# Moving the tiles of normed rows by 64 bytes in SBUF in a two-block transformer kernel

## The chip, the cores and the metric

The kernel runs on one core of one Trainium2 chip. The metric is the time of one execution on the device in microseconds, taken as the median of several runs.

## The reference

The input is a sequence of 256 rows of 1,024 numbers, all in 32-bit floating point. Two blocks follow one another, each with two layers of weights of its own.

```
def first_block(x, ...):
    for i in range(2):
        h = rms_norm(x, ln_attn_g[i])
        dq, dk, dv, mq, mk, mv = jnp.split(h @ w_in[i], cuts, axis=-1)
        ...
        x = x + jnp.concatenate([y_diff, y_moba], axis=-1) @ w_out[i]
        x = x + conv_ffn(rms_norm(x, ln_ffn_g[i]), w_up[i], conv_w[i], conv_b[i], w_down[i])
    return x

def second_block(x, c, ctx, ...):
    xc = ctx
    for l in range(2):
        h_l = _rmsnorm(x, g_pre[l]) * (1.0 + sc_l) + sh_l
        h_c = _rmsnorm(xc, g_pre[l]) * (1.0 + sc_c) + sh_c
        pl = _split_proj(h_l @ w_in[l])
        pc = _split_proj(h_c @ w_in[l])
        ...
        out_l = _mixer_output(pl, att_l, gla_l, *shared)
        if not last:
            out_c = _mixer_output(pc, att_c, gla_c, *shared)
            xc = xc + gt_c * _rmsnorm(out_c, g_post[l])
        x = x + gt_l * _rmsnorm(out_l, g_post[l])
    return x
```

In the first block `conv_ffn` multiplies the normed rows by `w_up` (1,024 by 5,632), applies a short convolution along the rows and a gated product, and multiplies by `w_down` (2,816 by 1,024). In the second block 256 rows of context go beside the 256 rows of the sequence through a wide projection into three branches (a convolution, an attention, a gated linear attention); in its second layer only the sequence's rows go on to the branches' outputs.

## The kernel before

Every large product is made on TensorE from numbers that were split in two: a number is rounded to the short form `float32r` (the "high" half), and the difference is the "low" half. A product is three matmuls: high by high, low rows by high weights, high rows by low weights.

Weights come in units of 512 KB (128 partitions by 1,024 numbers) by DMAs on SP's queue into the ring `RAW` (five slots). ScalarE rounds a unit into `SPH` (line 1559), and VectorE subtracts to make `SPL` (line 2132); both have four slots of 1,024 numbers. Rows are split into pairs of tiles:

- `HTH` and `HTL`, eight tiles (one per 128 of the 1,024 features) of 512 rows each, hold the normed rows, transposed, and later the attention output and the sum of the branches. With 256 rows in use, the slices are 256 columns long; with sequence and context together, 512.
- `ABH` and `ABL`, of the same shape, hold the inputs of the second block's branch products.
- `AH` and `AL`, three slots of 256 numbers, hold the gated product of the feed-forward stage, whose inner product with `w_down` is the function `down`.
- `RT` and `WDEC` are rows and weights of the low-rank decay product (line 1299).

Two functions of `tensor_program` make the products with HTH and HTL. `turned` (lines 1073 to 1075) loads a weight tile as the stationary side and streams 256 or 512 columns of rows, over eight tiles of features: 24 matmuls. `straight` (lines 1086 to 1088) loads 128 columns of rows as the stationary side and streams 512 columns of weights.

```
        for kt in kts:
            xh, xl = rows(src, kt)
            T.matmul(o, wh[:, kt, :], xh[:, kt, n0:n1], start=kt == 0, stop=False)
            T.matmul(o, wh[:, kt, :], xl[:, kt, n0:n1], start=False, stop=False)
            m = T.matmul(o, wl[:, kt, :], xh[:, kt, n0:n1], start=False, stop=kt == 7)
```

`down` (lines 1252 to 1254) does the same as `straight` with AH and AL as the stationary side, 12 matmuls for each of 22 tiles of features in each layer. In the profile's rows the tile that is named first after the arrow is the moving side, and the second is the stationary side. `rank` (lines 1263 and 1264) is a product of two of the three, with 512 columns.

Where a product's rows come from, `rows` decides (line 1052): HTH and HTL, or ABH and ABL for the three branch inputs. The order of the work on all engines is a list of steps that a planner writes ahead, from the program alone; addresses have no part in it.

The tiles' addresses are set in `build`: `put(name, off, shape)` places a tile at `base + off` in every partition, with `base` 16,512 (129 times 128), and returns the next free offset, rounded up to 32 bytes. RAW, SPH, SPL, HTH and HTL stand first, one behind the other, and all begin at a multiple of 128: SPH at 36,992, SPL at 53,376, HTH at 69,760, HTL at 86,144, each a multiple of 512 and 128 more. The offset `D` behind HTL is where all others are counted from. ABH stands at 188,224 and ABL at 204,608 (64 past a multiple of 128), AH at 212,832 and AL at 215,904 (96 past), RT at 204,608 and WDEC at 219,968 (64 past).

Of the kernel before, what the change touches and what calls it, by code (L numbers as in the profile page):

```python
# [7 lines left out]
F32R = mybir.dt.float32r  # L8
# [2829 lines left out]
def sync_program(sp, k):  # L2838
    D, sb, sched, s = sp.eng, k.sb, k.sched, k.signals

    def start():
        for t in range(2):
            D.dma_start(sb["XS"][:, t, 0:512], k.args["x"][0, t * 128:(t + 1) * 128, 0:512]).then_inc(
                *sp.tick(s["x_in0"]))

    def start2():
        for t in range(2):
            D.dma_start(sb["XS"][:, t, 512:1024], k.args["x"][0, t * 128:(t + 1) * 128, 512:1024]).then_inc(
                *sp.tick(s["x_in1"]))

    def load(u):
        name, idx, cols, kind = sched.order[u]
        p = u - NR
        if p >= 0 and sched.order[p][3] == "raw":
            sp.wait_ge(s["mm"], ("w", p))
        elif p >= 0:
            sp.wait_ge(s["hi"], ("u", p))
            sp.wait_ge(s["lo_" + sched.ready[p][1]], ("u", p))
        D.dma_start(sb["RAW"][:, u % NR, 0:cols], k.args[name][idx, :, 0:cols]).then_inc(
            *sp.tick(s[f"raw{u % NR}"], ("u", u)))  # L2860

    def finish():
        for t in range(2):
            for half, name in enumerate(("xa", "x")):
                c = slice(half * 512, half * 512 + 512)
                sp.wait_ge(s["out_dve"], (name, 1, t))
                D.dma_start(k.out[0, t * 128:(t + 1) * 128, c], sb["XS"][:, t, c]).then_inc(*sp.tick(s["out"]))
        sp.wait_ge(s["out"], 64)
        sp.wait_ge(s["spill0"], 32)
        sp.wait_ge(s["spill1"], 32)  # L2870

    does = {"start": start, "start2": start2, "load": load, "finish": finish}
    for step, *a in sched.steps:
        if step in does:
            does[step](*a)
# [6 lines left out]
def build(nc, args, out):  # L2882
    base = 16512
# [12 lines left out]
    m = Map()  # L2896
    o = m.put("RAW", 0, [128, 5, 1024])
    o = m.put("SPH", o, [128, 4, 1024], F32R)
    o = m.put("SPL", o, [128, 4, 1024], F32R)
    o = m.put("HTH", o, [128, 8, 512], F32R)  # L2900
    o = m.put("HTL", o, [128, 8, 512], F32R)
    D = o

    o = m.put("IDENT", D, [128, 128])
    o = m.put("PAR", o, [128, NPAR])
    o = m.put("TRI", o, [128, 384])
    o = m.put("MASK", o, [128, 7 * 128], U8)
    o = m.put("MODT", o, [128, 2, 24, 2])
    o = m.put("GP", o, [128, 2, 8, 2])
    o = m.put("CS", o, [128, 2, 16])  # L2910
    o = m.put("RS", o, [128, 3, 32])
    o = m.put("SS", o, [128, 8])
    o = m.put("GSS", o, [128, 2, 16])
    o = m.put("SSO", o, [128, 2, 4])
    o = m.put("AR", o, [128, 3, 4])
    o = m.put("ONE", o, [128, 1])
    o = m.put("BG", o, [128, 24])
    o = m.put("GC", o, [128, 2, 8])
    o = m.put("ROPE", o, [128, 2, 2, 2, 128])
    o = m.put("GN", o, [128, 2, 128])  # L2920
# [52 lines left out]
    p = m.put("YN", C + 16384, [128, 2, 1024])  # L2973
    p = m.put("QKN", p, [128, 2, 2, 512])
    p = m.put("VN", p, [128, 2, 1024])
    qkt_at = p
    p = m.put("QKT", p, [128, 8, 256])
    p = m.put("QP0", p, [128, 8, 256])
    p = m.put("BIAS", p, [128, 12, 256])
    m.put("MASKF", p, [128, 7 * 128])  # L2980
    p = m.put("E3", p, [128, 4, 384])
    m.put("DG1", p, [128, 2, 128])
    p = m.put("PT3", p, [128, 2, 384])
    p = m.put("XN1", p, [128, 2, 1024])
    p = m.put("SQ", p, [128, 2, 512])
    p = m.put("AROW1", p, [128, 256])
    p = m.put("SQY", p, [128, 512])
    p = m.put("QSY", p, [128, 2, 4])
    p = m.put("QS", p, [128, 2, 16])
    p = m.put("RR", p, [128, 4, 32])  # L2990
    p = m.put("SM", p, [128, 16])
    p = m.put("LT", p, [128, 64])
    p = m.put("LAMR", p, [128, 512])
    p = m.put("CSP", p, [128, 8, 32])
    p = m.put("SEL", p, [128, 2, 2])
    p = m.put("SE", p, [128, 2])

    m.put("FT", m.put("FC", qkt_at, [128, 2, 2, 256]), [128, 2, 256])
    p = m.put("AH", p, [128, 3, 256], F32R)
    p = m.put("AL", p, [128, 3, 256], F32R)  # L3000
    p = m.put("QP1", p, [128, 8, 256])
# [137 lines left out]
```

## Time and profile before

| | |
|---|---|
| median of 3 runs | 2103.14 us (2101.63 to 2103.3) |
| the profiled execution | 2102.27 us, span 2100.5 us |
| TensorE matmuls busy | 2053.5 us, 98% |
| TensorE weight loads busy | 1784.2 us, 85% |
| VectorE (DVE) busy | 1356.4 us, 65% |
| ScalarE (ACT) busy | 961.0 us, 46% |
| GpSimd (POOL) busy | 138.7 us, 7% |
| DMA | 285.79 MB, mean 136 GB/s |
| TensorE's granted clock | 0.994 of full speed |

The span goes from the first instruction to the last; the execution's time has a little at both ends beside it. Busy times of matmuls and weight loads overlap each other, and a matmul's duration holds a part in which the next one is already under way. So the price of a matmul in a dense stretch is read from the distance between the starts of two neighbours, in the timeline. By time, the stretches are: first block, layer 0 to 340 us and layer 1 to 680 us, each with projections and attention first and the feed-forward stage (147 to 340, 485 to 680) behind; second block, layer 0 to about 1560 us with 512 rows, and layer 1 from there with 256 rows in most products.

### The profile page before, as it was taken

The numbers are of one execution on the slowest core, as the hardware profiler recorded it, in microseconds if no ns is written. First come the engines' busy times: TensorE is split into PE (matmuls) and PEld (weight loads), VectorE is DVE, ScalarE is ACT, GpSimd is POOL, SyncE is SP. The second block draws the span as 40 slices with busy tenths as digits, with TensorE's granted clock in tenths as the row PEclk, the third lists the DMA queues.
The fourth block names the chain that finished last, engine by engine and source line by source line (L and its number), as shares of the span: only waits on it lengthen the run. The fifth ranks groups of instructions, "written<-read, shape, count | busy, mean of one in ns | idle before, by whom it ended". The sixth has DMA issues, their size and how long they took to land.

```text
span 2100.5 us, 31396 instructions
## 1 busy us (share of the span) xinstructions
PE 2053.5 (98%) x12082; PEld 1784.2 (85%) x12082; DVE 1356.4 (65%) x2381; ACT 961.0 (46%) x1576; POOL 138.7 (7%) x142
## 2 busy tenths in 40 slices
PE   9999999999999999999999999999999989999998
PEld 6788898878999888888888788888878889888997
DVE  6766667668777238567445556868565588575665
ACT  5655555655555434353332453233344454445443
POOL 1001000000110100000200001111110000100100
PEclk9999999999999999999999999999999999999999
DMA  8337656425555322112222104534234334251553
GB/s 262 134 131 270 223 205 210 161 101 173 184 181 188 122 99 71 65 66 81 71 90 91 61 26 158 193 108 160 91 121 159 102 120 141 97 175 60 192 171 131
DMA packets 79731, 285.79 MB, mean 136 GB/s; under 512 B 8976, under 2 KB 9628, under 8 KB 79584
## 3 DMA queue, kind: packets, MB, share of 16 engines
q1 hardware_dynamic: 71136, 256.93, 35.6%
q10 hardware_dynamic: 6416, 19.51, 2.5%
q0 software_dynamic: 2032, 7.35, 1.3%
q8 instruction: 97, 1.59, 0.3%
q14 instruction: 50, 0.41, 0.1%
HBM read 277.92 MB, written 5.83 MB: 135 GB/s over the span
## 4 chain that ended last, share of the span: by engine, by line
PE 85%; DVE 8%; ACT 4%; issue 2%; DMA 1%; POOL 0%; DVEq 0%; SPq 0%; ACTq 0%
PE pb L1073 16%; PE pb L1075 16%; PE pb L1074 16%; PE pb L1086 6%; PE pb L1088 6%; PE pb L1087 6%; PE pb L1092 3%; DVE SPL L2132 2%; PE pb L1252 2%; PE pb L1329 2%; PE pb L1253 2%; PE pb L1254 2%; PE pb L1432 2%; PE pb L1413 2%; ACT SPH L1559 1%
## 5 line engine op out<-in xcount | busy, mean ns | idle before, releaser
L2132 DVE TENSOR_TENSOR SPL<-RAW,SPH 128x1024 fp32r<-128x1024 f32 x460 | 560.0, 1232 | 396.5 <-ACT SPH L1559 372.2
L1073 PE MATMUL pb<-HTH,SPH 128*128 128x256 f32 (+1 forms) x2008 | 648.0, 323 | 12.6 <-DVE SPL L2132 6.2
L1075 PE MATMUL pb<-HTH,SPL 128*128 128x256 f32 (+1 forms) x2008 | 639.4, 318 | 0.0
L1074 PE MATMUL pb<-HTL,SPH 128*128 128x256 f32 (+1 forms) x2008 | 639.3, 318 | 0.0
L1559 ACT ACTIVATE SPH<-RAW 128x1024 fp32r<-128x1024 f32 x462 | 477.7, 1051 | 235.5 <-PE pb L1075 119.5
L1073 PEld LDWEIGHTS pb<-HTH,SPH 128*128 128x128 f32 x2008 | 384.4, 191 | 42.0 <-issue 8.6
L1074 PEld LDWEIGHTS pb<-HTL,SPH 128*128 128x128 f32 x2008 | 384.6, 192 | 26.6
L1075 PEld LDWEIGHTS pb<-HTH,SPL 128*128 128x128 f32 x2008 | 384.5, 191 | 26.0
L1086 PE MATMUL pb<-SPH,HTH 128*128 128x512 f32 x640 | 254.8, 398 | 0.8 <-DVE QNB L2573 0.5
L1088 PE MATMUL pb<-SPL,HTH 128*128 128x512 f32 x640 | 250.1, 391 | 0.0
L1087 PE MATMUL pb<-SPH,HTL 128*128 128x512 f32 x640 | 249.8, 390 | 0.0
L1086 PEld LDWEIGHTS pb<-SPH,HTH 128*128 128x128 f32 x640 | 120.8, 189 | 26.0 <-issue 1.3
L1088 PEld LDWEIGHTS pb<-SPL,HTH 128*128 128x128 f32 x640 | 120.4, 188 | 25.8
L1087 PEld LDWEIGHTS pb<-SPH,HTL 128*128 128x128 f32 x640 | 120.7, 189 | 23.8
L1073 PE MATMUL pb<-ABH,SPH 128*128 128x512 f32 (+1 forms) x384 | 130.7, 340 | 1.6 <-DVE SPL L2132 0.9
L1074 PE MATMUL pb<-ABL,SPH 128*128 128x512 f32 (+1 forms) x384 | 128.9, 336 | 0.0
L1075 PE MATMUL pb<-ABH,SPL 128*128 128x512 f32 (+1 forms) x384 | 128.8, 335 | 0.0
L1933 ACT ACTIVATE GT<-pb,BG 128x512 f32<-128x512 f32 (+1 forms) x48 | 27.8, 579 | 118.3 <-PE pb L1075 118.3
L1073 PEld LDWEIGHTS pb<-ABH,SPH 128*128 128x128 f32 x384 | 72.1, 188 | 10.9 <-issue 2.2
L1075 PEld LDWEIGHTS pb<-ABH,SPL 128*128 128x128 f32 x384 | 72.0, 188 | 8.8
L1074 PEld LDWEIGHTS pb<-ABL,SPH 128*128 128x128 f32 x384 | 72.1, 188 | 8.6 <-issue 0.2
L1252 PE MATMUL pb<-SPH,AH 128*128 128x512 f32 x176 | 71.6, 407 | 2.6 <-ACT SPH L1559 2.2
(286 smaller groups left out, 2491.8 us busy)
## 6 DMA issues: line engine op xcount, KB each, us to landing
RAW<-in_w_up SPq DMA_DIRECT2D x88, 512.0 KB, 4.5
RAW<-in_wa SPq DMA_DIRECT2D x64, 512.0 KB, 3.2
RAW<-in_w_in SPq DMA_DIRECT2D x48, 512.0 KB, 4.6
RAW<-in_wmg SPq DMA_DIRECT2D x48, 512.0 KB, 3.3
RAW<-in_wbr SPq DMA_DIRECT2D x48, 512.0 KB, 3.2
RAW<-in_w_down SPq DMA_DIRECT2D x44, 512.0 KB, 4.5
RAW<-in_w_ada SPq DMA_DIRECT2D x24, 512.0 KB, 4.5
ARAW<-in_w_ada ACTq DMA_DIRECT2D x24, 512.0 KB, 4.3
```

The source lines that it names most:

```text
L1073: T.matmul(o, wh[:, kt, :], xh[:, kt, n0:n1], start=kt == 0, stop=False)
L1074: T.matmul(o, wh[:, kt, :], xl[:, kt, n0:n1], start=False, stop=False)
L1075: m = T.matmul(o, wl[:, kt, :], xh[:, kt, n0:n1], start=False, stop=kt == 7)
L1086: T.matmul(P[:, :], xh[:, kt, c], wh[:, j, :], start=kt == 0, stop=False)
L1087: T.matmul(P[:, :], xl[:, kt, c], wh[:, j, :], start=False, stop=False)
L1088: m = T.matmul(P[:, :], xh[:, kt, c], wl[:, j, :], start=False, stop=kt == 7)
L1092: return T.transpose(o, i, ident)
L1252: T.matmul(P[:, :], xh, wh, start=j == 0, stop=False)
L1253: T.matmul(P[:, :], xl, wh, start=False, stop=False)
L1254: m = T.matmul(P[:, :], xh, wl, start=False, stop=end)
L1559: A.activation(hi, raw, ACT.Copy, scale=1.0).then_inc(*act.tick(s["hi"], ("u", u)))
L2132: W.tensor_tensor(lo, raw, hi.bitcast(F32), SUB).then_inc(*dve.tick(s["lo_dve"], ("u", u)))
```

## The change

The tiles HTH and HTL are put 64 bytes higher. What follows them is put 128 bytes higher in all, so that it keeps its place relative to a multiple of 128. Ahead of AH a gap is left so that AH, AL and QP1 start 64 past a multiple of 128, where they started 96 past one. No tile changes its size, and no instruction is added, removed or put elsewhere in its engine's order.

```diff
--- before.py
+++ after.py
@@ -2897,9 +2897,9 @@
     o = m.put("RAW", 0, [128, 5, 1024])
     o = m.put("SPH", o, [128, 4, 1024], F32R)
     o = m.put("SPL", o, [128, 4, 1024], F32R)
-    o = m.put("HTH", o, [128, 8, 512], F32R)
+    o = m.put("HTH", o + 64, [128, 8, 512], F32R)
     o = m.put("HTL", o, [128, 8, 512], F32R)
-    D = o
+    D = o + 64
 
     o = m.put("IDENT", D, [128, 128])
     o = m.put("PAR", o, [128, NPAR])
@@ -2996,6 +2996,7 @@
     p = m.put("SE", p, [128, 2])
 
     m.put("FT", m.put("FC", qkt_at, [128, 2, 2, 256]), [128, 2, 256])
+    p += (64 - base - p) % 128
     p = m.put("AH", p, [128, 3, 256], F32R)
     p = m.put("AL", p, [128, 3, 256], F32R)
     p = m.put("QP1", p, [128, 8, 256])
```

| tile | address before | after | past a multiple of 128, before | after |
|---|---|---|---|---|
| SPH, SPL | 36,992, 53,376 | the same | 0 | 0 |
| HTH, HTL | 69,760, 86,144 | 69,824, 86,208 | 0 | 64 |
| ABH, ABL | 188,224, 204,608 | 188,352, 204,736 | 64 | 64 |
| RT, WDEC | 204,608, 219,968 | 204,736, 220,096 | 64 | 64 |
| AH, AL | 212,832, 215,904 | 213,056, 216,128 | 96 | 64 |

## Rows read from the trace of the kernel before

**Rows 1.** The page of the profile: busy time by engine, and the chain's shares.
```profile
PE 2053.5 (98%) x12082; PEld 1784.2 (85%) x12082; DVE 1356.4 (65%) x2381; ACT 961.0 (46%) x1576; POOL 138.7 (7%) x142
...
PE 85%; DVE 8%; ACT 4%; issue 2%; DMA 1%; POOL 0%; DVEq 0%; SPq 0%; ACTq 0%
```

**Rows 2.** Groups by line and shape, TensorE: busy us, mean ns | idle before.
```profile
L1073 PE MATMUL pb<-HTH,SPH 128*128 128x256 f32 x1360 | 391.4, 288 | 12.6 <-DVE SPL L2132 6.2 <-POOL HTL L2774 2.7 <-DVE HTL L2217 1.5
...
L1073 PE MATMUL pb<-HTH,SPH 128*128 128x512 f32 x648 | 256.6, 396 | 0.0
L1086 PE MATMUL pb<-SPH,HTH 128*128 128x512 f32 x640 | 254.8, 398 | 0.8 <-DVE QNB L2573 0.5 <-ACT QP L1640 0.2
...
L1073 PE MATMUL pb<-ABH,SPH 128*128 128x512 f32 x192 | 76.5, 398 | 0.0
...
L1252 PE MATMUL pb<-SPH,AH 128*128 128x512 f32 x176 | 71.6, 407 | 2.6 <-ACT SPH L1559 2.2 <-issue 0.4
...
L1073 PE MATMUL pb<-ABH,SPH 128*128 128x256 f32 x192 | 54.3, 283 | 1.6 <-DVE SPL L2132 0.9 <-issue 0.5 <-DVE S L2605 0.2
```

**Rows 3.** Timeline, TensorE, 256 columns: start us, duration us, line, tiles.
```profile
299.45 0.28 PE L1073 MATMUL pb<-HTH,SPH 128*128 128x256 f32 x1
...
305.08 0.28 PE L1075 MATMUL pb<-HTH,SPL 128*128 128x256 f32 x1
...
1975.73 0.28 PE L1073 MATMUL pb<-HTH,SPH 128*128 128x256 f32 x1
...
1978.59 0.29 PE L1073 MATMUL pb<-ABH,SPH 128*128 128x256 f32 x1
...
1978.83 0.28 PE L1075 MATMUL pb<-ABH,SPL 128*128 128x256 f32 x1
...
1981.21 0.28 PE L1075 MATMUL pb<-ABH,SPL 128*128 128x256 f32 x1
...
1981.33 0.28 PE L1073 MATMUL pb<-HTH,SPH 128*128 128x256 f32 x1
```

**Rows 4.** Timeline, TensorE, 512 columns of rows as the moving side.
```profile
1047.37 0.39 PE L1073 MATMUL pb<-HTH,SPH 128*128 128x512 f32 x1
...
1052.81 0.39 PE L1073 MATMUL pb<-ABH,SPH 128*128 128x512 f32 x1
...
1058.41 0.39 PE L1073 MATMUL pb<-HTH,SPH 128*128 128x512 f32 x1
...
1063.87 0.39 PE L1073 MATMUL pb<-ABH,SPH 128*128 128x512 f32 x1
```

**Rows 5.** Timeline, TensorE, 512 columns of weights over stationary rows.
```profile
736.00 0.39 PE L1086 MATMUL pb<-SPH,HTH 128*128 128x512 f32 x1
...
779.52 0.39 PE L1073 MATMUL pb<-HTH,SPH 128*128 128x512 f32 x1
...
671.12 0.39 PE L1252 MATMUL pb<-SPH,AH 128*128 128x512 f32 x1
...
679.51 0.28 PE L1073 MATMUL pb<-HTH,SPH 128*128 128x256 f32 x1
```

**Rows 6.** Timeline, TensorE, the decay product, eight in one row.
```profile
782.24 1.11 PE L1299 MATMUL pb<-RT,WDEC 128*128 128x256 f32 x8
```

**Rows 7.** Busy us by stretch: length, PE, PEld, DVE, ACT, POOL (counts), granted clock.
```profile
20.00:147.00 127.00, 120.35 (x650) 99.65 (x648) 90.25 (x259) 71.72 (x148) 3.17 (x5) 0.99 0.53 161
340.00:485.00 145.00, 139.18 (x770) 114.74 (x768) 103.48 (x277) 83.44 (x168) 0.74 (x1) 0.99 0.48 162
147.00:340.00 193.00, 191.51 (x1404) 174.44 (x1403) 131.93 (x201) 103.40 (x155) 17.34 (x24) 1.00 0.62 219
1676.00:1706.00 30.00, 23.85 (x180) 23.67 (x179) 21.22 (x37) 18.33 (x22) 0.00 (x0) 0.89 0.37 122
1706.00:1770.00 64.00, 62.90 (x523) 62.46 (x522) 60.07 (x84) 26.28 (x34) 0.00 (x0) 1.00 0.38 125
```

**Rows 8.** The same by stretch, the instructions of line 1074 alone.
```profile
1706.00:1770.00 64.00, 35.54 (x127) 24.13 (x126) 1.00 0.38 125
```

## The prediction

> **What bounds the kernel now.** I read the busy times and the chain first, then the groups of instructions with their shapes kept apart, then TensorE's timeline for the distance between starts, then the busy times by stretch. TensorE is busy for 98% of the span and 85% of the chain that ended last lies on it [rows 1]; DVE, the next engine, has 65%. So a change in what one matmul costs goes into the end nearly one to one, except where TensorE waits. Most of its time is the three-product matmuls [rows 2]: 4,080 that stream 256 columns of HTH or HTL over weights (3 times 1,360), 1,944 that stream 512 columns of them (3 times 648), 1,920 that load HTH or HTL as the stationary side and stream 512 columns of weights (3 times 640), and 528 of the down projection with AH or AL stationary (3 times 176). Beside them stand 576 with 512 columns and 576 with 256 whose moving tile is ABH or ABL.
>
> The mean duration in those rows is no price, since matmuls overlap. The price is the distance from start to start in an undisturbed run. With 256 columns, 48 matmuls from HTH/HTL start from 299.45 to 305.08 us: 5.63 us over 47 distances is 119.8 ns [rows 3]. Late in the program runs of 24 alternate: HTH from 1975.73 to 1978.59, 119.2 ns each; then ABH, through the same function with the same weight slots, from 1978.59 to 1981.33, 114.2 ns each, and once settled (1978.83 to 1981.21, 21 distances) 113.3 ns [rows 3]. With 512 columns it is the other way round: HTH takes 5.44 us for 24, 226.7 ns, ABH 5.60 us, 233.3 ns, and the next HTH run, which begins unsettled, 5.46 us, 227.5 ns [rows 4]. With the rows stationary, HTH/HTL take 43.52 us for 192 matmuls, 226.7 ns, and AH/AL 8.39 us for 36, 233.1 ns [rows 5].
>
> **What the addresses have to do with it.** What differs between these pairs is where the tiles stand. I take the distance from the start of the stationary tile to the start of the moving one; all slices begin at multiples of 512 bytes, so it is the same for every matmul of a kind. For HTH/HTL with SPH/SPL it is a multiple of 512 before. For ABH (188,224) against SPH (36,992) it is 151,232 bytes, 64 past a multiple of 128 and 192 past one of 256. For SPH streamed over AH (212,832) it is 32 past a multiple of 128. A check on whether it is the distance or the address: RT over WDEC, both 64 past a multiple of 128, so at distance zero; their eight matmuls of 256 columns take 1.11 us, less one of 0.28 over seven distances 118.6 ns [rows 6], near HTH's 119.8 and not ABH's 113.3. So the working rule is: distance zero costs 120 at 256 columns and 226.7 at 512; a distance other than zero costs 113.3 and 233.3.
>
> The Trainium skill says otherwise: in SBUF — State Buffer, section Who interferes with whom, TensorE has two independent read ports, one for the moving side and one for weight loads, and never waits on anyone. By that, addresses could not matter and this change would give 0. The rows of the alternating runs disagree, by 5.0 ns a matmul.
>
> **The change part by part.** No instruction, wait, DMA or queue is added, removed or reordered; only addresses move. HTH and HTL move by 64 bytes, all that follows by 128, AH, AL and QP1 by 224. The engines that write these tiles do the same work. I cost that at nothing; it needs no cover.
>
> *256 columns from HTH/HTL.* The distance becomes 64, as ABH's modulo 128. The two feed-forward stages hold 2,112 of them (2 layers, 22 columns of tiles, 2 sides, 24 each), in runs of 48: I take 6.3 ns, just under the settled 6.5 (119.8 less 113.3): 13.3 us. The other 1,968 stand in shorter runs, between 5.0 (119.2 less 114.2) and 6.5; I take 5.7: 11.2 us. Together 24.5 us. Not all reaches the end. From 1706 to 1770 us DVE is busy for 60.07 of 64 us [rows 7], and 127 matmuls of one of the three lines, so 381, fall there [rows 8]: 2.2 us, of which I take 1.8 as lost, because DVE's mask, product and split steps are late next. From 1676 to 1706 TensorE is busy 23.85 of 30 us at a granted clock of 0.89 [rows 7], so it waits for others anyway: its 180 matmuls by 5.7 are 1.0 us, 0.7 lost. In the feed-forward stages (147 to 340 us) DVE is busy 131.93 of 193 us against TensorE's 191.51 [rows 7], so that gain passes. **Term: minus 22.0 us**; bounds 0 (if the new distance behaves like the old) and minus 26.5 (4,080 by 6.5, all passed).
>
> *512 columns from HTH/HTL.* 1,944 matmuls by 233.3 less 226.7, 6.6 ns settled; next to an unsettled run (227.5) it is 5.8. I take 6.0, as these stand mostly in runs of 24. **Plus 11.7 us**; bounds 0 and plus 12.8.
>
> *512 columns of weights over stationary HTH/HTL.* The two sides have changed places and the distance is now 64 before a multiple of 128. The only row with rows stationary and a distance other than zero is AH's 233.1, so I take the same 6.0 on 1,920: 11.5 us. In the first projections (20 to 147 and 340 to 485 us) TensorE is idle for 6.65 and 5.82 us [rows 7], in waits for weights and norms that slower matmuls use up in part: I take 1.0 off. **Plus 10.5 us**; bounds 0 and plus 12.7 (1,920 by 6.6).
>
> *AH/AL.* From distance 32 to 64. Both are other than zero, and the rows give 233.1 for the one and 233.3 for the other: nothing. Bounds plus and minus 3.5 us (528 by the 6.6 between the two levels). ABH/ABL keep their distance modulo 128: nothing, if 128 is what counts.
>
> **Sum:** minus 22.0, plus 11.7, plus 10.5: plus 0.2 us on the profiled execution's 2102.27, which is 2102.5. That execution lies 0.87 below the median of the three runs, 2103.14, so against the median it would be 2103.3. I forecast 2103, no change that can be told; its own range is 2098 to 2108, from the tiles at the bounds of AH and half a nanosecond on the 4,080 and the 3,864. About 0.2%, 4.2 us, is what a measurement of this kernel can tell from no change.
>
> **The rivals.** *Faster: the long matmuls do not pay.* My rule rests on 128 as the period. If it is 256, ABH's distance is 192, and HTH's new one as the moving side, 64, stands in no row; only the stationary case has ABH's 192 and its known price. Then the 256-column gain may come without the 512-column moving cost: minus 22.0 plus 10.5 is minus 11.5, 2090.8 us. If stationary rows are spared as well (AH's 233 may come from its 32, which is no multiple of 64): minus 22.0, 2080.3. For it: the two settled levels of ABH go in opposite directions, which a single conflict does not explain, so the two need not move together. Against: the price of 233 appears at both distances other than zero that the trace has, on either side.
>
> *Slower: the short matmuls do not gain.* One mechanism, the same period of 256 with the other outcome: the streamed HTH at distance 64 stays at 120 with 256 columns, while stationary HTH stands at 192, where ABH paid. Plus 10.5: 2112.8. If the 512-column moving matmuls pay too, plus 22.2: 2124.5. It decides as soon as the 256-column distance after the change is over 117, half of the gain. For it: 24 us of gain rest on one pair of tiles. Against: that pair has 576 matmuls and differs in nothing else that I can see.
>
> *Nothing happens.* Not the low bits but how far apart the tiles lie may count: ABH, ABL, AH and AL all stand above 188,000, SPH to HTL below 102,600. Then 64 bytes do nothing: 2102.3. RT and WDEC, both far up, at 118.6, fit this as well. By the skill's two ports it would be this too.
>
> **How the numbers follow.** Forecast 0.42, of which 0.04 falls beyond 0.2% on either side; nothing happens 0.08; faster 0.28, half for each price; slower 0.22, 0.12 for the half price and 0.10 for the full. So faster 0.32, same 0.42, slower 0.26. The range goes from 2079, which takes in 2080.3, to 2117, which takes in 2112.8; the full slower case and a little on each side are left out.
>
> **What would show it.** In the changed kernel's timeline: 256-column runs from HTH at 113 to 114 ns, 512-column runs at 233 with HTH on either side, AH's and ABH's unchanged at 233, ABH's 256 at 113. In the busy times by stretch the feed-forward stages are shorter by some 6.5 us each, the mixer's first layer longer by about as much in sum, and 1706 to 1770 hardly shorter. HTH at 120 with 256 columns, or at 227 with 512, would make the prediction wrong, by the term concerned; so would AH or ABH at any level other than today's.

## The result, and the profile after

The changed kernel takes 2107.39 us in the median of 16 runs (2104.7 to 2111.14) against 2104.0 of the kernel before, measured beside it (2101.63 to 2107.25): a ratio of 1.0015, interval 1.0008 to 1.0022. So it is 3.4 us slower. That lies in the forecast's own 2098 to 2108 and within the 0.2% named there, but the interval of sixteen runs of each leaves out 1, so the loss is real. All times here are of executions at the usual clock; one execution of a kernel below, at a mean granted clock of 0.654, took 2889.41 us and is left out. The profiled execution took 2107.18 us, its span 2105.4 against 2100.5.

First the page: busy time by engine, and the shares of the chain of waits.

```profile
PE 2057.3 (98%) x12082; PEld 1776.7 (84%) x12082; DVE 1355.5 (64%) x2381; ACT 961.2 (46%) x1576; POOL 138.9 (7%) x142
...
PE 81%; DVE 11%; ACT 5%; issue 2%; DMA 1%; DVEq 0%; POOL 0%; ACTq 0%; SPq 0%
```

The same engine bounds it, as busy as before [rows 1]. Then the groups by line and shape, those of [rows 2] (busy us, mean ns | idle before).

```profile
L1073 PE MATMUL pb<-HTH,SPH 128*128 128x256 f32 x1360 | 385.1, 283 | 13.2 <-DVE SPL L2132 6.6 <-POOL HTL L2774 2.9 <-DVE HTL L2217 1.5
...
L1073 PE MATMUL pb<-HTH,SPH 128*128 128x512 f32 x648 | 259.0, 400 | 0.0
L1086 PE MATMUL pb<-SPH,HTH 128*128 128x512 f32 x640 | 258.4, 404 | 0.5 <-DVE QNB L2573 0.5
...
L1073 PE MATMUL pb<-ABH,SPH 128*128 128x512 f32 x192 | 76.3, 398 | 0.0
...
L1252 PE MATMUL pb<-SPH,AH 128*128 128x512 f32 x176 | 72.1, 410 | 2.7 <-ACT SPH L1559 2.6
...
L1073 PE MATMUL pb<-ABH,SPH 128*128 128x256 f32 x192 | 54.7, 285 | 2.2 <-DVE SPL L2132 1.1 <-issue 0.9 <-DVE S L2605 0.2
```

The idle time ahead of each group, and what ended it, is that of before to within 0.6 us: no new wait. With 256 columns HTH's mean is lower (288 to 283 ns), with 512 it is higher on either side (396 to 400, 398 to 404), and ABH's has moved as well, up with 256 columns (283 to 285). The prices stand in TensorE's timeline (start us, duration us, line, tiles); its rows answer to [rows 3 to 5]. A price is called settled when it is taken behind the first few matmuls of a run, whose distances still differ from those that follow.

```profile
298.56 0.28 PE L1073 MATMUL pb<-HTH,SPH 128*128 128x256 f32 x1
...
304.09 0.28 PE L1075 MATMUL pb<-HTH,SPL 128*128 128x256 f32 x1
...
670.94 0.40 PE L1252 MATMUL pb<-SPH,AH 128*128 128x512 f32 x1
...
679.21 0.28 PE L1073 MATMUL pb<-HTH,SPH 128*128 128x256 f32 x1
...
734.24 0.39 PE L1086 MATMUL pb<-SPH,HTH 128*128 128x512 f32 x1
...
779.04 0.40 PE L1073 MATMUL pb<-HTH,SPH 128*128 128x512 f32 x1
...
1049.60 0.40 PE L1073 MATMUL pb<-HTH,SPH 128*128 128x512 f32 x1
...
1055.20 0.40 PE L1073 MATMUL pb<-ABH,SPH 128*128 128x512 f32 x1
...
1095.28 0.39 PE L1073 MATMUL pb<-HTH,SPH 128*128 128x512 f32 x1
...
1100.79 0.39 PE L1073 MATMUL pb<-ABH,SPH 128*128 128x512 f32 x1
...
1106.28 0.39 PE L1073 MATMUL pb<-HTH,SPH 128*128 128x512 f32 x1
...
1753.38 0.28 PE L1074 MATMUL pb<-HTL,SPH 128*128 128x256 f32 x1
...
1758.59 0.28 PE L1075 MATMUL pb<-HTH,SPL 128*128 128x256 f32 x1
...
1976.62 0.28 PE L1073 MATMUL pb<-ABH,SPH 128*128 128x256 f32 x1
...
1979.44 0.28 PE L1073 MATMUL pb<-HTH,SPH 128*128 128x256 f32 x1
```

- HTH with 256 columns: 5.53 us over 47 distances, 117.7 ns, not 113.3 [rows 3]. Only a few runs reach that level: from 1753.38 to 1758.59 us 46 distances, 113.3.
- ABH with 256 columns: 2.82 us for 24, 117.5 ns (117.8 settled in the trace), where [rows 3] had 113.3. Its distance modulo 128 has not changed.
- Stationary HTH: 44.80 us for 192, 233.3 ns, as forecast [rows 5].
- HTH moving, 512 columns: 5.60 us for 24 at 1049.60, 233.3 ns; 5.51 at 1095.28, 229.6, and most runs settle at 229. ABH's next run, 5.49 us, 228.8, has become cheaper than its 233.3 [rows 4].
- AH: 8.27 us for 36, 229.7 ns, for 233.1 [rows 5].

To see what each kind is worth, I set the 12,082 matmuls of the two traces beside each other in their order, which is the same, and took for each kind the change in the distance to the next start (a wait behind a matmul counts with it). One thing has to be kept apart. TensorE's granted clock is 2.4 GHz in nearly all of both spans, but 1.2 GHz in some short stretches, and these do not all lie at the same place in the two traces. One falls into the down product of the changed kernel. In the timeline, before and then after the change:

```profile
513.54 0.47 PE L1252 MATMUL pb<-SPH,AH 128*128 128x512 f32 x1 [1.84 <-ACT SPH L1559]
...
514.24 0.47 PE L1252 MATMUL pb<-SPH,AH 128*128 128x512 f32 x1 [2.20 <-ACT SPH L1559]
```

and the same stretch of both as busy times, read as [rows 7] (the clock as a share of 2.4 GHz is the number ahead of the last two):

```profile
514.90:518.20 3.30, 3.30 (x23) 2.98 (x22) 3.19 (x7) 0.42 (x1) 0.00 (x0) 1.00 0.90 312
...
514.90:518.20 3.30, 3.30 (x10) 2.53 (x9) 3.23 (x7) 0.42 (x1) 0.00 (x0) 0.50 0.84 237
```

In both traces TensorE waited for SPH, for 1.84 and for 2.20 us, and went on with the down product; behind the wait the clock fell in one of them alone. Why there is not shown. So the 129 distances that touch a stretch at 1.2 GHz in either trace have a column of their own.

| kind | matmuls | forecast us | measured us | ns each | beside it, at 1.2 GHz, us |
|---|---|---|---|---|---|
| 256 columns, HTH/HTL moving | 4,080 | -22.0 | -7.3 | -1.8 | -3.3 |
| 512 columns, HTH/HTL moving (with `rank`) | 1,976 | +11.7 | +3.5 | +1.8 | +0.6 |
| 512 columns, HTH/HTL stationary | 1,919 | +10.5 | +10.0 | +5.2 | +1.2 |
| 512 columns, ABH/ABL | 576 | 0 | -2.25 | -3.9 | 0 |
| 256 columns, ABH/ABL | 576 | 0 | +2.2 | +3.8 | 0 |
| AH/AL stationary | 528 | 0 | -1.55 | -3.0 | +1.6 |
| all others | 2,426 | 0 | +0.3 | | -0.1 |
| sum | | +0.2 | +4.9 | | 0.0 |

That is the 4.9 us by which the spans differ; the medians of 16 differ by 3.4. Were the last column counted in, HTH's 256 columns would seem to gain 3.3 us more, and AH nothing at all. Where a change "by kind" is given below, it is made in this way against the profiled execution of before, 2102.27 us, with what lies at 1.2 GHz in either trace left out.

### The profile page after: what moved, and what is told of

Same layout as the page of the kernel before. It is cut to its first block, busy times and chain, and to the rows that moved or that the text cites. A ratio compares the mean times of both kernels' runs of the same rounds, so it can differ in the third digit from the quotient of the medians.

```text
span 2105.4 us, 31396 instructions
## 1 busy us (share of the span) xinstructions
PE 2057.3 (98%) x12082; PEld 1776.7 (84%) x12082; DVE 1355.5 (64%) x2381; ACT 961.2 (46%) x1576; POOL 138.9 (7%) x142
## 4 chain that ended last, share of the span: by engine, by line
PE 81%; DVE 11%; ACT 5%; issue 2%; DMA 1%; DVEq 0%; POOL 0%; ACTq 0%; SPq 0%
PE pb L1073 15%; PE pb L1075 15%; PE pb L1074 15%; PE pb L1086 6%; PE pb L1088 6%; PE pb L1087 6%; DVE SPL L2132 3%; PE pb L1092 3%; ACT SPH L1559 2%; PE pb L1252 2%; PE pb L1329 2%; PE pb L1254 2%; PE pb L1253 2%; PE pb L1432 2%; PE pb L1413 2%
## 5 line engine op out<-in xcount | busy, mean ns | idle before, releaser
L1559 ACT ACTIVATE SPH<-RAW 128x1024 fp32r<-128x1024 f32 x462 | 477.9, 1052 | 238.7 <-PE pb L1075 117.1
L1073 PEld LDWEIGHTS pb<-HTH,SPH 128*128 128x128 f32 x2008 | 377.9, 188 | 42.2 <-issue 9.2
L1075 PEld LDWEIGHTS pb<-HTH,SPL 128*128 128x128 f32 x2008 | 377.7, 188 | 28.0
L1074 PEld LDWEIGHTS pb<-HTL,SPH 128*128 128x128 f32 x2008 | 377.9, 188 | 27.4
L1933 ACT ACTIVATE GT<-pb,BG 128x512 f32<-128x512 f32 (+1 forms) x48 | 27.8, 579 | 118.6 <-PE pb L1075 118.6
L1073 PEld LDWEIGHTS pb<-ABH,SPH 128*128 128x128 f32 x384 | 72.2, 188 | 10.4 <-issue 2.8
```

Source lines behind the costliest of these rows:

```text
L1559: A.activation(hi, raw, ACT.Copy, scale=1.0).then_inc(*act.tick(s["hi"], ("u", u)))
```

## The experiments

Theory D: the distance counts, but modulo 256, counted from the start of the stationary tile to that of the moving one, and each distance has its own level. Before, HTH stands at 0, ABH at 192, AH at 32; after, at 64, 64 and 64, and HTH as the stationary side at 192, the distance at which ABH paid 233.3 before. Rivals: P, the period is 128 and something else spoils the gain; T, not the distance but the tile or its part of the memory counts; others are named where they come. Where no ratio is given, the kernel was executed once; single executions of the kernel before lie between 2101.38 and 2107.83 us, so such a time tells only differences larger than that.

**HTH at 128, ABH at 0, AH at 0.** The two tiles change places as far as D goes; by P, HTH stands as before.

```diff
-    o = m.put("HTH", o, [128, 8, 512], F32R)
+    o = m.put("HTH", o + 128, [128, 8, 512], F32R)
     o = m.put("HTL", o, [128, 8, 512], F32R)
-    D = o
+    D = o + 192
...
+    p += (128 - base - p) % 256
     p = m.put("AH", p, [128, 3, 256], F32R)
```

> HTH and HTL stand 128 bytes past SPH (modulo 256), ABH and ABL at 0, AH and AL at 0. Theory D (the price of a matmul hangs on the distance between its moving and its stationary tile modulo 256 and on nothing else): ABH takes HTH's prices of before, 120 ns at 256 columns and 226.7 at 512, and AH's matmuls fall from 233 to 226.7; HTH streamed and HTH stationary show one and the same level at 512 columns, since 128 and minus 128 are one distance. Theory P (a period of 128, as in the prediction): HTH shows 120 and 226.7 as before, AH 226.7, ABH 120 and 226.7. Theory T (the tile, or how far up it stands, sets it): ABH stays at 113 to 118 and 229 to 233, AH at 230 to 233.

Measured: 2120.78 us against 2104.21. The timeline of this kernel:

```profile
293.93 0.28 PE L1073 MATMUL pb<-HTH,SPH 128*128 128x256 f32 x1
...
299.56 0.29 PE L1075 MATMUL pb<-HTH,SPL 128*128 128x256 f32 x1
...
1057.77 0.40 PE L1073 MATMUL pb<-HTH,SPH 128*128 128x512 f32 x1
...
1063.37 0.39 PE L1073 MATMUL pb<-ABH,SPH 128*128 128x512 f32 x1
...
1309.06 0.39 PE L1073 MATMUL pb<-ABH,SPH 128*128 128x512 f32 x1
...
1319.73 0.39 PE L1075 MATMUL pb<-ABH,SPL 128*128 128x512 f32 x1
```

ABH at 0 takes 10.67 us over 47 distances, 227.0 ns: HTH's old price, on the tile that had 233.3. HTH at 128 takes 5.60 us for 24, 233.3, with 512 columns, and with 256 still 119.8 (5.63 over 47). T falls by the one, P by the other: 128 is not 0. In the trace HTH settles at 232.0 to 233.6 with 512 columns, moving or stationary, as D has it for 128 and minus 128. AH at 0 settles at 226.7 as well (the last 24 of the 36 matmuls from 676.76 us), but most of its pieces are 12 long and begin unsettled, at 224 to 236, so it gains 1.6 us and not the 3.4 of its full level. The change by kind: stationary +9.6, HTH 512 +9.6, HTH 256 -1.1, ABH -3.3 and +3.1, AH -1.6.

**HTH at 192, ABH at 128, AH at 192.** HTH takes ABH's old distance.

```diff
-    o = m.put("HTH", o, [128, 8, 512], F32R)
+    o = m.put("HTH", o + 192, [128, 8, 512], F32R)
...
+    p += (192 - base - p) % 256
     p = m.put("AH", p, [128, 3, 256], F32R)
```

> HTH and HTL stand 192 bytes past SPH (modulo 256), where ABH stood before; ABH at 128, AH at 192 counted from the stationary to the moving tile. Theory D: streamed HTH takes ABH's prices of before, 113.3 ns at 256 columns and 233.3 at 512; HTH stationary is then at minus 192, that is 64, and costs 229 (or 233, the second level that the changed kernel shows now and then); ABH shows what HTH showed at 128; AH stays at 233. From the 256 columns minus 6.5 by 4,080, minus 26.5 us, from the 512 streamed plus 12.8, from the stationary plus 4.4: some 9 us less than before, 2094. Theory P: like the changed kernel, so about 117.8 at 256 columns and 229 at 512 with HTH streamed. Theory T: HTH differs from before only by having been moved, so like the changed kernel too.

Measured: 2104.09 against 2104.21.

```profile
287.47 0.28 PE L1073 MATMUL pb<-HTH,SPH 128*128 128x256 f32 x1
...
292.81 0.28 PE L1075 MATMUL pb<-HTH,SPL 128*128 128x256 f32 x1
...
1044.08 0.39 PE L1073 MATMUL pb<-HTH,SPH 128*128 128x512 f32 x1
...
1049.68 0.39 PE L1073 MATMUL pb<-ABH,SPH 128*128 128x512 f32 x1
```

5.34 us over 47 is 113.6 ns, 5.60 for 24 is 233.3: HTH at 192 has both of ABH's old levels, so what the prediction hoped for at 64 does come at 192. But about a third of its runs of 256 columns (28 of the 86 with 24 matmuls or more) stay near 118. By kind: HTH 256 -14.5, HTH 512 +10.6, stationary (at 64) +3.2, ABH +2.4, AH +0.1, others +1.2. D has the levels right and the sum, 9 us less, wrong: a third of the runs, and ABH at 128, gave it back.

**HTH at 32 and HTH at 224.** The same places again, for more of the map (ABH at 96 and 160, AH at 128 and 96).

```diff
-    o = m.put("HTH", o, [128, 8, 512], F32R)
+    o = m.put("HTH", o + 32, [128, 8, 512], F32R)
     o = m.put("HTL", o, [128, 8, 512], F32R)
-    D = o
+    D = o + 128
...
+    p += (0 - base - p) % 256
```

```diff
-    o = m.put("HTH", o, [128, 8, 512], F32R)
+    o = m.put("HTH", o + 224, [128, 8, 512], F32R)
...
+    p += (32 - base - p) % 256
```

> HTH and HTL stand 32 bytes past SPH, so HTH stationary is at 224; ABH at 96, AH at 128. Theory D: streamed HTH at 512 columns costs 233, as AH at distance 32 did before; AH at 128 costs what HTH costs at 128 in the kernel with that distance. Levels at 256 columns for 32 and at 96 and 224 are not known yet. Theory P: HTH at 32 as at 160, AH back at 226.7. Theory T: AH at 230 to 233 whatever its distance, HTH as in the changed kernel.

> HTH and HTL stand 224 bytes past SPH, so HTH stationary is at 32; ABH at 160, AH at 96. Theory D: HTH stationary costs 233, as AH at 32 did before; streamed HTH at 512 columns costs what HTH stationary costs in the kernel with 32; AH at 96 costs what ABH at 96 costs there. Theory P: 160 and 32 alike, 224 and 96 alike. Theory T: ABH and AH as ever, 113 to 118, 229 to 233.

Measured: 2113.46 and 2119.82 against 2104.21. A run of 48 with HTH at 32, and one at 224:

```profile
289.31 0.28 PE L1073 MATMUL pb<-HTH,SPH 128*128 128x256 f32 x1
...
294.80 0.28 PE L1075 MATMUL pb<-HTH,SPL 128*128 128x256 f32 x1
...
291.83 0.28 PE L1073 MATMUL pb<-HTH,SPH 128*128 128x256 f32 x1
...
297.39 0.28 PE L1075 MATMUL pb<-HTH,SPL 128*128 128x256 f32 x1
```

At 32 that is 5.49 us over 47, settled 116.7 ns in the trace, and 233.4 with 512 columns; at 224 it is 5.56 over 47, 118.3, and 233.3; stationary, which is at 224 in the one and at 32 in the other, 233.3 and 233.4. By kind, at 32: HTH 256 -9.2, HTH 512 +10.3, stationary +9.6, ABH +3.3, AH -0.5; at 224: -4.8, +10.4, +10.0, +2.7, AH 0. The gain with 256 columns is a part, the cost with 512 is whole.

**HTH by 64 alone,** ABH kept at 192 and AH at 32.

```diff
-    o = m.put("HTH", o, [128, 8, 512], F32R)
+    o = m.put("HTH", o + 64, [128, 8, 512], F32R)
     o = m.put("HTL", o, [128, 8, 512], F32R)
-    D = o
+    D = o + 192
```

> HTH and HTL alone move by 64 bytes; what stands behind them moves by 256, so ABH stays at 192 and AH at 32 modulo 256. Theory D (distance modulo 256): all of the change's loss and gain with HTH is here: 4,080 by minus 2.2 is minus 9, 1,944 by plus 2.3 is plus 4.5, 1,920 stationary by some 5.5 is plus 10.5, so some 6 us slower than before, ratio 1.003; ABH back at 113.3 and 233.3, AH at 233.4. Rival Q (moving ABH and AH is what made the changed kernel slower): no slower than before.

Measured: 2108.16 against 2103.16, ratio 1.0025 (1.0016 to 1.0034). Its timeline:

```profile
1997.05 0.28 PE L1073 MATMUL pb<-HTH,SPH 128*128 128x256 f32 x1
...
1999.88 0.28 PE L1073 MATMUL pb<-ABH,SPH 128*128 128x256 f32 x1
...
2002.60 0.28 PE L1073 MATMUL pb<-HTH,SPH 128*128 128x256 f32 x1
```

HTH 2.83 us for 24, 117.9 ns; ABH 2.72, 113.3. ABH at 192 has its old level, so in the changed kernel it was ABH's move from 192 to 64 that took it away: the period is not 128. It is not 512 either: here ABH stands 448 past a multiple of 512 and before the change 192, with the same two levels, and in the changed kernel HTH (64) and ABH (320) share theirs. By kind: stationary +10.0, HTH 256 -6.3, HTH 512 +3.9, ABH +0.35, AH 0: the change's cost is that of moving HTH. D's levels hold, and the rival named there, Q, falls.

**SPH, SPL, HTH and HTL all by 64:** new addresses, HTH's distance still 0 (ABH 128, AH 96).

```diff
-    o = m.put("SPH", o, [128, 4, 1024], F32R)
+    o = m.put("SPH", o + 64, [128, 4, 1024], F32R)
...
-    D = o
+    D = o + 192
```

> SPH, SPL, HTH and HTL all stand 64 bytes higher, 64 past a multiple of 128: the distance between HTH and SPH is 0 as before, the address is not. ABH and AH move by 256, so their distances to SPH become 128 and 96. Theory D: HTH 120 ns at 256 columns and 226.7 at 512 on both sides, ABH as in the kernel with ABH at 128 (119, 232.7), AH 233; time within 6 us of before. Rival A (the address of HTH itself modulo 128 decides): HTH at 117.8 and 229 to 233 as in the changed kernel.

Measured: 2105.18 against 2103.16.

```profile
290.58 0.28 PE L1073 MATMUL pb<-HTH,SPH 128*128 128x256 f32 x1
...
296.22 0.28 PE L1075 MATMUL pb<-HTH,SPL 128*128 128x256 f32 x1
...
723.99 0.39 PE L1073 MATMUL pb<-HTH,SPH 128*128 128x512 f32 x1
...
736.23 0.39 PE L1086 MATMUL pb<-SPH,HTH 128*128 128x512 f32 x1
...
740.99 0.39 PE L1086 MATMUL pb<-SPH,HTH 128*128 128x512 f32 x1
```

5.64 us over 47 is 120.0. With 512 columns, 12.24 us for 54 moving and 4.76 for 21 stationary are 226.7 each: the levels of distance 0, at addresses 64 higher. It is the distance, not the address, and rival A falls.

**A better placement.** The map says: 256 columns want 192, 512 columns want 0. The first layer's feed-forward rows (tag `f0`, 1,056 matmuls of 256 columns) are only a moving side, so a second pair of tiles, HSH and HSL, is laid over HTH and HTL 192 bytes higher for them.

```diff
+def normed(sb, tag):
+    s = tag == "f0"
+    return (sb["HSH"], sb["HSL"]) if s else (sb["HTH"], sb["HTL"])
...
-        return HH, HL
+        return normed(sb, src[0])
...
+    m.put("HSH", o - 16384 + 192, [128, 8, 512], F32R)
+    m.put("HSL", o + 192, [128, 8, 512], F32R)
     o = m.put("HTL", o, [128, 8, 512], F32R)
-    D = o
+    D = o + 256
```

> Only the normed rows of the first layer's feed-forward stage stand at distance 192, in tiles laid over HTH and HTL; all other uses of HTH and HTL are at 0, ABH at 192, AH at 32 as before. Theory D: 1,056 matmuls of 256 columns go from 120 to 113.3, some runs of 48 lock at 117.8 instead: between 2.3 and 7 us faster than before, nearer 6, all of it between 147 and 340 us of the trace, nothing slower. Rival S (a gain in the feed-forward stage does not reach the end, since DVE or the DMAs set its pace): no faster than before by more than 2 us, with the distance of 113.3 in the trace all the same and idle time between runs.

Measured: 2100.51 against 2103.16, ratio 0.9987 (0.9978 to 0.9997). Of the 21 runs at 192, 9 are at 113.5 ns, 12 at 117.8. By kind these 1,056 matmuls gain 4.0 us, their waits counted, and no other kind changes by more than 0.8: the gain reaches the end, and rival S falls.

Then the second mixer layer's rows (`x1`, `c1`) at 192 as well, the first mixer layer's branch inputs at 0 (tiles ASH and ASL, 64 past ABH and ABL), and AH at 0:

```diff
-    s = tag == "f0"
+    s = tag in ("f0", "x1", "c1")
...
-            return (HH, HL) if w == "s" else (ABH, ABL)
+            return (HH, HL) if w == "s" else (ABH, ABL) if l else (sb["ASH"], sb["ASL"])
...
+    m.put("ASH", Z + 64, [128, 8, 512], F32R)
-    e = m.put("ABL", Z + 16384, [128, 8, 512], F32R)
+    m.put("ABL", Z + 16384, [128, 8, 512], F32R)
+    e = m.put("ASL", Z + 16384 + 64, [128, 8, 512], F32R)
...
+    p += (128 - base - p) % 256
     p = m.put("AH", p, [128, 3, 256], F32R)
```

> Each use at the distance that its matmuls like best: 256 columns at 192 (the first layer's feed-forward rows, the normed rows of the mixer's second layer, ABH there), 512 columns at 0 (HTH elsewhere, ABH in the mixer's first layer, AH). Theory D: minus 6 from the feed-forward stage, minus 7 from the mixer's second layer (1,968 by 4.5 with some of it lost to DVE), minus 3.5 from ABH's 576 at 512 columns, minus 1.8 from AH, plus 0.5 from stationary rows at minus 192: some 18 us faster than before, ratio 0.991; at least 10 us faster if more runs lock at 117.8. If distance were not what sets the price: no change.

Measured: 2095.49 against 2103.16, ratio 0.9965 (0.9952 to 0.9977): faster than both kernels, but not by the sum expected. By kind: HSH 256 -6.8, ASH 512 -3.5, AH -2.4, but HSH as the stationary side +1.8 and with 512 columns +1.2 (its 112 of these were in no term), ABH 256 +1.5 (still at 192, but with most of its runs at the upper level now), HTH stationary, not moved, +0.8, others +1.2. To part it, the same without `x1` and `c1`, and these alone (without the lines on ASH, ASL and AH):

```diff
-    s = tag in ("f0", "x1", "c1")
+    s = tag == "f0"
```

```diff
-    s = tag in ("f0", "x1", "c1")
+    s = tag in ("x1", "c1")
```

> The first layer's feed-forward rows at 192, the first layer's branch inputs and AH at 0, everything else at its old distance; the second mixer layer's rows go back from 192 to 0. The distance theory, with the levels as the last runs show them: 256 columns from the feed-forward rows about -6 us by their spacing, branch inputs with 512 columns -3.5, with 256 columns +1 to +2, AH -1: about -9 us in spacing, 2094, ratio 0.995 to 0.997; the stationary rows all at 227. If the parts overlap as they did in the last mixture, where about 5 us of sums expected did not come, it stays at 0.9965 or above.

> Only the second mixer layer's normed rows (sequence and context) at 192, through the second pair of tiles; all else at its old distance. The distance theory: their 256-column matmuls at 113.4 or 117.8, about half of the runs at each, -3 us; the same rows as the stationary side stand at minus 192, which is 64: 229 to 233 for 227, +2 to +4. In sum -1 to +2 us, ratio 0.9995 to 1.001. A rival, that the stationary side is not charged where the rows are those of the second layer: -3 us, 0.9985.

Measured: without them 2095.38 against 2104.59, ratio 0.9959 (0.9946 to 0.9973); they alone 2103.78 in the median of nine, ratio 0.9996 (0.9987 to 1.0006). So by its times that part is worth nothing that can be told. By kind its 256 columns gain 5.4 us, and the same rows cost 1.6 as the stationary side, at 64, and 0.8 with 512 columns: the stationary side is charged, and the rival that spared it falls. The timeline of the kernel without it:

```profile
287.32 0.39 PE L1259 MATMUL pb<-SPL,AH 128*128 128x512 f32 x1
287.55 0.28 PE L1078 MATMUL pb<-HSH,SPH 128*128 128x256 f32 x1
...
293.08 0.28 PE L1080 MATMUL pb<-HSH,SPL 128*128 128x256 f32 x1
...
1290.31 0.39 PE L1078 MATMUL pb<-ASH,SPH 128*128 128x512 f32 x1
...
1301.19 0.39 PE L1078 MATMUL pb<-HTH,SPH 128*128 128x512 f32 x1
```

ASH at 0 takes 10.88 us for 48, 226.7 ns, where ABH at 192 took 233.3. But HSH at 192 takes 5.53 us over 47, 117.7: all 19 of its runs behind a piece of the down product are at the upper level, where with AH at 32 9 were at the lower.

**What decides which level a run takes.** With AH at 32, the 9 runs at 113.5 stood behind a matmul of the down product that had started 233 or 234 ns ahead, the 10 at 117.8 behind one of 226 to 232; with AH at 0, all behind 226 or 227. Two kernels in which, beside the last one, nothing is moved but AH with what stands behind it:

```diff
-    p += (128 - base - p) % 256
+    p += (192 - base - p) % 256
     p = m.put("AH", p, [128, 3, 256], F32R)
```

```diff
-    p += (128 - base - p) % 256
+    p += (32 - base - p) % 256
     p = m.put("AH", p, [128, 3, 256], F32R)
```

> As the mixture of the first layer's feed-forward rows at 192, its branch inputs at 0 and AH at 0, but with AH at 192. There, 19 of the 19 runs of 48 behind a piece of the down product locked at 117.8, and the last matmul of that piece stood 226 or 227 ns ahead of the run. Theory L (a run at 192 takes its level over from the matmul ahead of it): in the earlier kernels every run behind a matmul that stood 233 to 236 ns ahead was at 113.5, every run but one behind 226 to 231 at 117.8. With AH at 192, where the down product ends mostly on 233 to 236, some three quarters of the 19 lock at 113.5: 256 columns -2.5 to -3 us beside the mixture, while AH's 512 columns cost 233.3 for 227.5, +3 us: the time as the mixture's, ratio 0.9955 to 0.997. Rival R (the level is fixed by where the tiles of the run itself stand, and which one comes is chance or code fetch): 2 to 3 of 21 as in the mixture or half as before, not tied to the spacing of the matmul ahead; with the former +3 us over the mixture.

> The same with AH at 96, where an earlier kernel's down product had a mean of 233.6 but ended on 229 to 231 ns ahead of every feed-forward run. Theory L: where the last spacing is 226 to 231, the runs at 192 stay at 117.8 although the down product's mean is near 233; any that end on 233 to 236 lock at 113.5. Theory M (it is the mean level of the down product ahead, 233, that counts): most of the 19 lock at 113.5. Rival R: no tie to either.

Measured: AH at 192, 2095.66 against 2104.55, ratio 0.9957 (0.994 to 0.9974); AH at 96, 2092.05 in one execution. The timeline with AH at 96:

```profile
286.06 0.39 PE L1259 MATMUL pb<-SPL,AH 128*128 128x512 f32 x1
286.29 0.28 PE L1078 MATMUL pb<-HSH,SPH 128*128 128x256 f32 x1
...
291.62 0.28 PE L1080 MATMUL pb<-HSH,SPL 128*128 128x256 f32 x1
```

5.33 us over 47, 113.4 ns, behind a matmul that started 229 ns ahead (in the trace's whole ns). In the table, the mean of the down product leaves out the first four matmuls of a piece.

| AH at | mean distance in the down product, ns | runs of `f0` behind it at the lower level | start of the last matmul ahead of these, ns | of those at the upper level |
|---|---|---|---|---|
| 0 | 227.5 | 0 of 19 | none | 226, 227 |
| 32 | 233.4 | 9 of 19 | 233, 234 | 226 to 232 |
| 192 | 233.3 | 12 of 19 | 235, 236 | 229, 230 |
| 96 | 233.3 | 19 of 19 | 228 to 231 | none |

These means hide a pattern: at 192 the distances are 231 and 236 ns in turn, at 96 they are near 231, 231 and 238, so which is the last depends on where a piece ends. Rival R falls: which level a run takes follows from where the tile of the product ahead stands; between the kernels with AH at 0, 192 and 96 nothing was moved but AH and what stands behind it. (The one at 32 has other branch inputs, which come only later.) There is one trace of each; the kernel with `x1` and `c1` at 192, where AH is at 0 too, has 0 of 19 as well. Theory L holds at 0, 32 and 192, run for run, but falls at 96: the last spacing is a sign of what is handed over, not the thing itself. Theory M names 0 and 96 and misses 32 and 192, where the same mean leaves the runs divided. What is handed over stays open. Little time is won by it: by kind, with AH at 96 the 256 columns gain 3.8 us more than with AH at 0, and the down product costs 2.5 more; the one execution, 2092.05, lies beside the 2092.27 to 2097.23 of AH at 0.

## Why the prediction came out as it did

**Where the bound lies: right.** TensorE's spacing makes the difference; the seven kinds in the table sum to the spans' difference, and the stretch from 147 to 340 us is as full as in [rows 7]:

```profile
147.00:340.00 193.00, 191.72 (x1425) 174.99 (x1424) 133.06 (x203) 105.93 (x161) 17.34 (x24) 1.00 0.63 225
```

**The distance decides, and not the address: right.** This was read from RT and WDEC [rows 6], which was weaker than it looked, since 118.6 is also near the levels that 128 and 224 turned out to have; it is now shown by moving all four tiles together. Why the distance counts, no run here shows. The Trainium skill (SBUF — State Buffer, section Who interferes with whom) gives the two sides independent read ports. By that nothing would have moved; the runs disagree, by up to 16.6 us of 2104 with HTH at 128. "Nothing happens" is excluded too: all but 0.3 us of the 4.9 lie in the kinds whose distance changed.

**"A distance other than zero costs 113.3 and 233.3": the step that failed.** It made one class of all distances but zero, with 128 as the period, from two of them in the trace (ABH's and AH's). The period is 256, so ABH's distance was 192, and 64 stood in no row, as the rivals said and the sum did not heed. The terms:

- *256 columns, minus 22.0:* -7.3 came. The settled gain at 64 is about 2 ns (119.8 to 117.7), not 6.3, but for the few runs at the lower level.
- *512 columns moving, plus 11.7:* +3.5 came. At 64 most runs settle near 229, with some at 233.3.
- *512 columns stationary, plus 10.5:* +10.0 came. HTH on this side stands at 192, which the trace had priced for 512 columns, by ABH.
- *ABH, nothing:* -2.25 and +2.2. It moved from 192 to 64 and took on 64's levels. That the two cancel was luck.
- *AH, nothing:* its settled level fell by 3.4 ns (233.1 to 229.7 [rows 5]), and 1.55 us came back. From 32 to 64 is no move within one class: 64 has a price of its own on this side too.

Two errors of opposite sign, 14.7 us short of the gain and 8.2 short of the cost, make 6.5; AH gave back 1.55 and the rest 0.25, which leaves the 4.7 by which the sum was off. That the time still fell into 2098 to 2108 is luck: both large terms with HTH moving were wrong by more than half.

**The rivals.** Both rested on the true premise, the period of 256. The slower one set its point at 117 ns with 256 columns: 117.7 is beyond it, and slower it came, with the stationary term as priced. Its 2112.8 overshot since 64 is neither the old level nor the other: both kinds went about a third of the way. The faster one asked that the long matmuls pay nothing; they paid a third, and the stationary side in full.

**What it takes to gain.** The same terms with the right map: feed-forward rows at 192, branch inputs and AH at 0 gave 0.9959 (0.9946 to 0.9973). The second feed-forward layer's rows at 192 in this way were not tried: in the trace of before, ScalarE writes the next rows, those of the context, into HTH from 535.2 to 598.2 us, while TensorE still reads these.

## What to carry to other kernels

Where every matmul has its own weight load, as in this kernel, look at the distance of the two operands' tiles modulo 256, and read its price for each length from the timeline, since one distance can be good for 256 columns and bad for 512. A distance that no row shows is unknown, not equal to its neighbour: move one tile and measure. A term that rests on a period should be written down with the next longer period beside it. Before two traces are set beside each other by kinds, take out the stretches at the lower clock: here they hid AH's gain and made HTH's look larger.

## What the runs showed that was not expected

Start to start, settled, by distance modulo 256 (all kernels above; for the stationary rows the distance counts in the same direction, from the stationary tile to the moving one):

| distance | 256 columns, ns | 512 columns, ns |
|---|---|---|
| 0 | 120 | 226.7 |
| 32 | 116.7 | 233.4 |
| 64 | 117.8, some runs 113.3 | 229, some runs 233.3 |
| 96 | 119.9 | 233.5 |
| 128 | 118.7 to 120 | 232 to 233.6 |
| 160 | 117.1 to 118.9 | 234.3 |
| 192 | 113.4, some runs 117.8 | 233.3 |
| 224 | 118.3 | 233.3 |

Two things in it were not expected: a period of 256, with 0 alone cheap for 512 columns and 192 for 256; and two levels at the same distance, of which a run takes one at its start and keeps it to its end, unless a wait interrupts it (the run of 180 from 1680.10 us of the changed kernel is at 113.3 ahead of its wait and at 117.8 behind it). Which one, follows from the work ahead of it, as the four places of AH show; by what, is open.
